# A joined change: 256-key neighbourhood units, transposed router logits, one second matrix loaded ahead of its ring

## Chip, core and metric

The program runs on one core of a Trainium2 chip, in one launch. The metric is the device time of that launch in microseconds. TensorE is called PE, VectorE DVE, ScalarE ACT, GpSimd POOL and SyncE SP. Everything is 32-bit float. The core has 16 DMA engines, which all queues share.

## What is computed

A first block on 512 tokens of width 1024 (normed attention of two kinds, an output projection, a mixture of 32 experts, a side path), and then two more layers with a context of 256 tokens, which the change doesn't touch. What matters here, cut from the reference:

```python
ob = neighbourhood_attention(...)   # 16 heads of 32; 8 rows of 64 columns; a query sees all 8 rows,
    kb = np.minimum(cs[:, 0], GRID_W - K_COLS)      # K_COLS = 32 columns per block of 16 query columns
    key_cols = kb[:, None] + np.arange(K_COLS)[None, :]
    col_valid = ((key_cols[:, None, :] >= cs[:, :, None]) & (key_cols[:, None, :] < cs[:, :, None] + WIN_C))
    sc = einsum(qb, kg) * scale + bias;  pr = softmax(sc);  o = einsum(pr, vg)
h = h + concatenate([oa, ob]) @ w_out
g_prob = softmax(xf @ w_rg);  g_gate, g_idx = top_k(g_prob, 1)      # 4 groups
e_logits = (xf @ w_re)[group g_idx];  e_w, e_i = top_k(softmax(e_logits), 2)   # 8 experts in each
hdn = silu(xb @ w1[e]) * (xb @ w3[e]);  y = hdn @ w2[e]             # 1024 x 512, 1024 x 512, 512 x 1024
h = h + rms_norm(p @ w_ple, g_ple) * sigmoid(rms_norm(h, g_plg) @ w_plg)
```

## The kernel before

The tokens are ordered so that one tile of 128 tokens is a block of 16 grid columns by 8 rows; there are XT = 4 tiles. The first layer (`first_layer`, tensors named `mix_...`) runs in stages, and each engine has its instructions written out by hand in one list, with semaphores between the lists.

**Attention.** The class `Attention` writes one attention for all engines. A unit is one tile of queries of one group of heads. PE's list for iteration n (`tensor`): scores of unit n+LEAD, where a group begins soon its turned q and k (L338), transposes of unit n's weights (L377, in pieces of four tiles), a turned output of the first attention (`extra`, L403), turned inverses of a group that has closed (L411), values of unit n-1 (L391; L394 in the first attention). DVE (`vector`) takes each head's maximum with the bias added (L504), copies every piece but the first (L208) and finishes a group. ACT (`scalar`) copies the first piece (L208), then makes the exponentials of unit n+LEAD, one per head (L587), then empties an extra (L454). Three PSUM banks go round for all that is turned. `diff` is the first attention (16 units of 512 keys, LEAD 2, two score maps), `near` the neighbourhood attention: four groups of four heads, 16 units, LEAD 1. Its units of tiles 0 and 3 see two tiles of keys (256), those of tiles 1 and 2 three tiles (384). The bias blocks, which also mask the columns outside the window, are built by POOL from the padded table (`shifted`), written to `bias_blocks` in HBM by ACT's queue, and read by SP's queue into EM, two groups' worth of room, 8 transfers a group (L897, `table_in`).

**Behind it.** PE projects with w_out (L1031), turns h (L1041), multiplies by the router's matrix (`route`, L1047: the turned h of a tile is stationary, w_router's 36 columns move), and does pieces of the side product p @ w_ple (`beside`, L1085, eight of two products each) between the ranking (L1092, L1094) and the two slot lists (L1103). DVE scales the logits (L1591) and chooses groups and experts (L1616 to L1631). POOL gathers expert rows (L1901) and scatters results (L1908).

**Experts.** 31 experts run in a fixed loop, the last and any overflow in a dynamic one (one trip here). PE's list for expert e: first product w1 (L1138), hidden of e-1 turned (L1143), product w3 (L1138), rows of e+1 turned (L1131), second product of e-1 with w2 (L1150). Each matrix has 2 MB. SP loads them in the order of use into six places, `use_of(which, e) % PLACES`; a load waits until the matrix six uses back has been read. The sixth place is the tensor `sixth` and part of `consts`, in three transfers (L920 to L922); others take one (L924). From expert 7 on pieces of the context layer run along, for which ACT's queue loads 12 x 0.5 MB. What the change touches of the memory: `base` (EM, and the context's rows in the same range), `work` (q, k, weights, later the router's h), `sixth`, and the place of the side norm (`own`, `side_gain`).

Below, w1(e), w3(e), w2(e) are an expert's matrices.

## Time and profile before

| | us |
|---|---|
| median of three runs | 1813.12 (1813.02 to 1815.79) |
| the profiled execution | 1818.79 |
| its span | 1817.0 |
| input projection, to 205.6 | 205.6 |
| first attention | 48.7 |
| neighbourhood attention, 254.3 to 320.5 | 66.2 |
| output projection | 55.5 |
| router and slot lists | 35.4 |
| experts, 411.4 to 920.1 | 508.7 |
| the two later layers | 896.9 |
| PE busy over the span | 1752.2 (96%) |

In the page, the span is cut into 40 slices of 45.4 us: transfers move 393 to 419 GB/s in the eleven slices from 409 to 908 us and at most 286 elsewhere. PE busy is modelled from pipelined matmuls, so 96% doesn't say that it can't go faster; what it waits for is read in its waits and in the timeline. The clock column (PEclk) is the share of 2.4 GHz that was granted; 0.50 means 1.2 GHz.

### The profile page before, as it was taken

The page shows a single profiled execution, that of the slowest core. Times are in us where ns is not written, and L with a number is a line of the kernel's source. Part 1 is how long each engine was busy: PE and PEld are TensorE (multiplying, and loading weights), DVE is VectorE, ACT ScalarE, POOL GpSimd, SP SyncE. Part 2 cuts the span into 40 slices and gives each one's busy share as a digit, 9 for nine tenths or more (in the row PEclk, how much of TensorE's full clock was granted, in tenths as well). Part 3 has the DMA queues.
Part 4 walks back from the last instruction along what each step waited for, and adds up shares of the span by engine and source line. Part 5 has one row for each costly group of instructions (what it writes and reads, how often), then busy time and mean ns, then how long its engine had stood idle before and what let it go on. Part 6 is the DMA issues. An engine that isn't in the chain of part 4 may idle for free. (4 is left out here: it accounts for less than half of the span.)

```text
span 1817.0 us, 24698 instructions
## 1 busy us (share of the span) xinstructions
PE 1752.2 (96%) x9850; PEld 971.7 (53%) x9850; DVE 748.2 (41%) x1591; ACT 555.0 (31%) x1121; POOL 153.8 (8%) x194
## 2 busy tenths in 40 slices
PE   8999988999999899999989999999999999999998
PEld 3443455465544444555474444577745644566663
DVE  2344477132511221333223315477624337566642
ACT  2111477123101111333223212355412233444420
POOL 0310000001111010111100014000000001100000
PEclk9999999989999999999999999999999999999999
DMA  8664688439999999999971222000110012100001
GB/s 282 229 223 185 94 163 117 165 124 393 417 416 416 415 416 417 418 417 419 409 286 47 93 93 93 1 2 1 36 73 35 24 41 74 43 1 2 2 24 47
DMA packets 94594, 324.86 MB, mean 179 GB/s; under 512 B 12792, under 2 KB 31224, under 8 KB 69392
## 3 DMA queue, kind: packets, MB, share of 16 engines
q1 hardware_dynamic: 80624, 302.55, 45.7%
q10 hardware_dynamic: 8656, 12.32, 2.0%
q0 software_dynamic: 5200, 8.41, 1.3%
q8 instruction: 79, 1.29, 0.3%
q14 instruction: 35, 0.29, 0.1%
HBM read 317.58 MB, written 14.30 MB: 183 GB/s over the span
## 5 line engine op out<-in xcount | busy, mean ns | idle before, releaser
L2228 PE MATMUL tail_ps<-arena 128*128 128x512 f32 x488 | 213.3, 592 | 0.0
L1138 PE MATMUL mix_ps<-arena 128*64 128x256 f32 x1568 | 181.8, 385 | 8.3 <-DMA arena<-in_w 5.8
L1014 PE MATMUL mix_ps<-arena,side 128*128 128x512 f32 x384 | 171.1, 603 | 1.2 <-DMA arena<-in_w_in 0.6
L500 DVE TENSOR_SCALAR_CACHE_REDUCE arena<-tail_ps 128x768 f32<-128x768 f32 x128 | 117.5, 955 | 114.2 <-PE tail_ps L358 69.8
L2228 PEld LDWEIGHTS tail_ps<-arena 128*128 128x128 f32 x488 | 91.8, 190 | 110.3 <-issue 109.9
L1138 PEld LDWEIGHTS mix_ps<-arena 128*64 128x64 f32 x1568 | 110.3, 138 | 70.3 <-issue 11.8
L1150 PE MATMUL mix_ps<-arena 128*64 128x512 f32 x512 | 116.9, 598 | 18.9 <-DMA arena<-in_w 18.3
L1014 PEld LDWEIGHTS mix_ps<-arena,side 128*128 128x128 f32 x384 | 72.7, 192 | 97.4 <-issue 94.9
L2228 PE MATMUL tail_ps<-arena,side 128*128 128x512 f32 (+2 forms) x328 | 123.6, 535 | 0.0
L587 ACT ACTIVATE arena<-arena,tail_small 128x768 f32<-128x768 f32 x128 | 118.0, 926 | 6.4 <-DVE arena L500 6.4
L377 PE MATMUL tail_ps<-first,arena 128*128 128x128 f32 x768 | 97.9, 277 | 0.5 <-ACT arena L587 0.5
L377 PEld LDWEIGHTS tail_ps<-first,arena 128*128 128x128 f32 x768 | 82.7, 140 | 28.1 <-issue 26.8
L2228 PEld LDWEIGHTS tail_ps<-arena,side 128*128 128x128 f32 x328 | 61.9, 190 | 58.1 <-issue 47.4
L1400 ACT ACTIVATE arena<-mix_ps,mix_small 128x512 f32<-128x512 f32 x31 | 21.3, 687 | 226.2 <-PE mix_ps L1150 226.2
L1684 DVE COPY arena<-mix_ps 128x256 f32<-128x256 f32 x31 | 13.1, 424 | 180.3 <-PE mix_ps L1143 180.2
L2228 PE MATMUL tail_ps<-side,arena 128*128 128x512 f32 x184 | 80.4, 592 | 0.0
L1150 PEld LDWEIGHTS mix_ps<-arena 128*64 128x64 f32 x512 | 34.1, 136 | 78.8 <-issue 55.5
L1908 POOL DMA_INDIRECT expert_out<-arena,mix_indices x31 | 31.5, 1016 | 413.7 <-ACT arena L1400 407.3
L1336 ACT ACTIVATE arena<-mix_ps,mix_small 128x512 f32<-128x512 f32 x24 | 16.2, 687 | 149.9 <-PE mix_ps L1014 128.5
L2228 PEld LDWEIGHTS tail_ps<-side,arena 128*128 128x128 f32 x184 | 34.9, 190 | 43.5 <-issue 43.5
L1138 PE MATMUL mix_ps<-sixth,arena 128*64 128x256 f32 x450 | 54.8, 382 | 0.6 <-issue 0.6
L1031 PE MATMUL mix_ps<-arena,side 128*128 128x512 f32 x128 | 55.3, 592 | 0.0
(411 smaller groups left out, 2458.5 us busy)
## 6 DMA issues: line engine op xcount, KB each, us to landing
arena<-in_w SPq DMA_DIRECT2D x81, 2048.0 KB, 18.3
arena<-in_l_w_mod SPq DMA_DIRECT2D x16, 1024.0 KB, 6.5
arena<-in_l_w_in SPq DMA_DIRECT2D x16, 1024.0 KB, 7.2
sixth<-in_w SPq DMA_DIRECT2D x15, 1024.0 KB
sixth<-in_w SPq DMA_DIRECT2D x15, 896.0 KB
arena<-in_w_in SPq DMA_DIRECT2D x12, 1024.0 KB, 9.2
arena<-in_l_w_mod SPq DMA_DIRECT2D x16, 512.0 KB, 6.1
residual<-bias_blocks SPq DMA_DIRECT2D x32, 224.0 KB, 12.2
```

The source lines that it names most:

```text
L377: ins = pe.transpose(Tp[:, bank, z * P:(z + 1) * P], pr[:, n % self.PRB, x, kt * P:(kt + 1) * P], m["ident"])
L500: dve.tensor_scalar(self.rows_of(n, x), self.scores_of(n, x), -1.0, None, ALU.mult, ALU.min, accum_out=nm[:, b, x:x + 1]).then_inc(s["maxe ...
L587: act.activation(pr[:, b, x, 0:k], in_, ACT.Exp, bias=nm[:, b, x:x + 1], scale=scale, accum_out=sm[:, og_b, z, x:x + 1]).then_inc(s["exped ...
L1014: last = pe.matmul(ps[:, u % 4], oT[:, k, t * P:(t + 1) * P], weights.slot(W_IN[n, k // 4], 4, 512)[:, k % 4], start=(k == 0), stop=(k == ...
L1031: last = pe.matmul(ps[:, u % 4], oT[:, k, t * P:(t + 1) * P], weights.slot(W_OUT[cc, k // 4], 4, 512)[:, k % 4], start=(k == 0), stop=(k = ...
L1138: last = pe.matmul(out[h * CAP:(h + 1) * CAP, 0:H2], x, block_of(k, h), start=(k == 0), stop=(k == DK - 1))
L1150: last = pe.matmul(py[h * CAP:(h + 1) * CAP, :], x, wb[:, f, h * 512:(h + 1) * 512], start=(f == 0), stop=(f == FK - 1))
L1336: act.activation(proj[:, t, cc * 512:(cc + 1) * 512], ps[:, (XT * n + t) % 4], ACT.Copy, scale=rs_x[:, t:t + 1]).then_inc(s["in_ev"], 1)
L1400: act.activation(yb[:, e % 2], py, ACT.Copy, scale=gate_w[:, e:e + 1]).then_inc(s["y_out"], 1)
L1684: dve.tensor_copy(hT.rearrange("p j q -> p (j q)"), ph[:, 0:2 * P]).then_inc(s["h_taken"], 1)
L1908: pool.indirect_dma_start(out=y_rows, out_offset=bass.IndirectOffsetOnAxis(ap=index[:, 1, e:e + 1], axis=0), in_=yb[:, e % 2], in_offset=N ...
L2228: last = pe.matmul(out, lhs(k), rhs(k), start=(k == 0), stop=(k == K - 1))
```

## The change

- **Units of 256 keys.** The units of tiles 1 and 2 take the half tile on either side and their own tile, 256 keys instead of 384. The keys are read in place by a strided pattern (`near_keys`); their scores are made in two products of 128 keys for each head (`cut`). The outer halves of the values are put together beforehand by 32 transfers of 8 partitions x 512 on SP's queue (`mixed`), for which the second unit's values wait. A bias table has 24 blocks instead of 28.
- **Order inside the attention.** ACT makes the exponentials of n+1 ahead of the copy of n's weights (`ahead`). The first group's q and k are turned inside the first attention, at its unit 14 (`turns_after`). The turned outputs come at units 7, 8, 11, 12 instead of 5, 7, 9, 11.
- **Tables.** The third group's table goes into the sixth place and no longer waits for the first group; the fourth waits for the first group's maxima. w1(2), which goes into the sixth place too, is loaded behind the third group's maxima.
- **Router.** w_router is stationary and h moves: one product chain for tiles 0 and 1, one for each of tiles 2 and 3; DVE copies the logits (36 partitions), PE turns them, DVE scales them in one instruction.
- **Side product.** Piece 5 stands behind the second slot list; pieces 6 and 7 stand in expert 0 behind its third step.
- **Ring.** w2(1) is loaded once into `once`, outside the ring, right behind the router's norms; the context's rows follow. The order of use is a list (`asked`), so the odd place is now filled by w3 of even experts. The side norm (own squares, gain) runs one expert later, its row `g_ple` is loaded at expert 4.

The diff, cut to its core:

```diff
@@ Attention
-            cuts = [(a, min(hi - lo, a + 4)) for a in range(0, hi - lo, 4)]
+            cuts = [(a, min(hi - lo, a + self.cut(t))) for a in range(0, hi - lo, self.cut(t))]
...
+        if turns_after is not None:
+            self.turn_step[turns_after[0]] = (self.groups, range(len(turns_after[1])))
...
+            if self.ahead and n + LEAD < self.N:
+                exponential(n + LEAD)
             if n < self.N:
                 self.empty_weights(act, 1, n)
-            if n + LEAD < self.N:
+            if not self.ahead and n + LEAD < self.N:
                 exponential(n + LEAD)
...
@@ first_layer
+    bias_at = [EM[:, 0], EM[:, 1], view(sixth, 0, 24, P), EM[:, 0]]
+    TABLE_IN = ((0, 2), (0, 2), (1, 1), (0, 3))
...
+    def near_keys(g, x, t, lo, hi):
+
+        rows_of_head = slice(32 * x, 32 * x + 32)
+        if not middle(t):
+            first = 0 if t == 0 else (XT - 2) * P
+            return kT[rows_of_head, g % 2, first + (lo - 2 * t) * P:first + (hi - 2 * t) * P]
+        if lo == 2 * t + 1:
+            return kT[rows_of_head, g % 2, t * P:(t + 1) * P]
+        both = view(work, 1024 + g % 2 * SEQ + (t - 1) * P + CB // 2, 2, 2 * P - CB // 2)[rows_of_head, :, 0:P]
+        return both.rearrange("p h (r c) -> p h r c", c=CB)[:, :, :, 0:CB // 2].rearrange("p h r c -> p r h c")
...
             for g in range(2):
                 table_in(g)
+            sp.wait_ge(s["in_ev"], 24)
+            for t in range(1, XT - 1):
+                for half in range(2):
+                    for r in range(ROWS):
+                        to, of = r * CB + half * (CB // 2), r * CB + (1 - half) * (CB // 2)
+                        sp.dma_start(mixed[to:to + CB // 2, t - 1], proj[of:of + CB // 2, t - 1 + 2 * half, 2560:3072]).then_inc(s["mixed_in"], 16)
             for i in range(W_OUT[0, 0], W_PLE + 1):
                 weights.load(sp, i)
-            for g in range(2, 4):
-                sp.wait_ge(s["near_maxed"], near.first_of[g - 1] * 4)
-                table_in(g)
+            table_in(2)
+            sp.wait_ge(s["near_maxed"], near.first_of[1] * 4)
+            table_in(3)
...
-            sp.wait_ge(s["shifted"], 1)
+            sp.wait_ge(s["near_maxed"], near.first_of[3] * 4)
             expert(2, "w1")
...
             expert(1, "w3")
+            sp.wait_ge(s["h_squared"], 2 * XT)
+            expert(1, "w2")
+            for b in range(2):
+                sp.wait_ge(s["spilled"][b], 32)
+            sp.dma_start(hx[:, XT:AT], A["ctx"].rearrange("(t p) d -> p t d", p=P)).then_inc(s["ctx_in"], 16)
             sp.wait_ge(s["listed"], 2)
             expert(0, "w2")
...
+            def route(i):
+                lo, hi = route_parts[i]
+                pe.wait_ge(s["h_gained"], hi)
                 for k in range(DK):
-                    last = pe.matmul(ps[:, t, 0:N_GROUPS + N_EXPERTS], h_in[:, k, t * P:(t + 1) * P], wr[:, k], start=(k == 0), stop=(k == DK - 1))
+                    last = pe.matmul(ps[0:WIDTH, i, 0:(hi - lo) * P], wr[:, k], h_in[:, k, lo * P:hi * P], start=(k == 0), stop=(k == DK - 1))
+                last.then_inc(s["logits"], 1)
...
                 if e:
                     second(e - 1)
+                else:
+                    beside(6)
+                    beside(7)
```

In the order of instructions, three places. ACT's list inside the neighbourhood attention, one group from its turned keys to its first output. L587 and L595 are exponentials, L208 copies what PE turned, L454 and L461 empty a turned output of the first attention. Before:

```order
L208 ACTIVATE arena<-mix_ps 128x512 x2
L587 ACTIVATE arena,mix_small<-arena,mix_small 128x256 x4
L208 ACTIVATE arena<-mix_ps 128x512
L587 ACTIVATE arena,mix_small<-arena,mix_small 128x256 x4
L454 ACTIVATE side<-mix_ps,mix_small 128x512
L208 ACTIVATE arena<-mix_ps 128x512
L587 ACTIVATE arena,mix_small<-arena,mix_small 128x384 x4
```

After:

```order
L208 ACTIVATE arena<-mix_ps 128x512 x2
L595 ACTIVATE arena,mix_small<-arena,mix_small 128x256 x4
L208 ACTIVATE arena<-mix_ps 128x512
L595 ACTIVATE arena,mix_small<-arena,mix_small 128x256 x4
L208 ACTIVATE arena<-mix_ps 128x512
L461 ACTIVATE side<-mix_ps,mix_small 128x512
L595 ACTIVATE arena,mix_small<-arena,mix_small 128x256 x4
```

The alternation reads the same, but a copy is now that of the unit before the exponentials above it, not of the one whose exponentials follow; and no row has 384 keys.

PE's list from the last turning of h to the first expert. L1047 and L1105 are the router's products, L1111 the turned logits, L1085 and L1149 the side product, L1103 and L1167 the slot lists, L1131 and L1193 an expert's rows, L1138 and L1200 its first products. Before, first the router and then, further down, the lists:

```order
L1041 MATMUL mix_ps<-first,residual 128x128 x16
L1047 MATMUL mix_ps<-arena 128x36 x16
L1041 MATMUL mix_ps<-first,residual 128x128 x8
L1047 MATMUL mix_ps<-arena 128x36 x16
L1085 MATMUL mix_ps<-arena,extra 128x512 x6
...
L1103 MATMUL mix_ps<-arena 128x32 x8
L1085 MATMUL mix_ps<-arena,extra 128x512 x4
L1103 MATMUL mix_ps<-arena 128x64 x8
L1085 MATMUL mix_ps<-arena,extra 128x512 x4
L1131 MATMUL mix_ps<-first,arena 128x128 x4
```

After:

```order
L1098 MATMUL mix_ps<-first,residual 128x128 x16
L1105 MATMUL mix_ps<-arena 36x256 x8
L1098 MATMUL mix_ps<-first,residual 128x128 x8
L1105 MATMUL mix_ps<-arena 36x128 x16
L1111 MATMUL mix_ps<-first,arena 128x36 x4
...
L1149 MATMUL mix_ps<-arena,extra 128x512 x2
L1167 MATMUL mix_ps<-arena 128x64 x8
L1149 MATMUL mix_ps<-arena,extra 128x512 x2
L1193 MATMUL mix_ps<-first,arena 128x128 x4
L1200 MATMUL mix_ps<-arena 64x256 x32
L1193 MATMUL mix_ps<-first,arena 128x128 x4
L1149 MATMUL mix_ps<-arena,extra 128x512 x4
```

Two side products left the space between the lists, two that before the first rows, and four products (pieces 6 and 7) stand behind the second expert's turned rows.

SP's queue from the first tables on. Before:

```order
L897 DMA residual<-bias_blocks 16x28x128 x16
L650 DMA arena<-in_w_out 128x4x512 x4
L650 DMA arena<-in_w_ple 128x2x1024
L897 DMA residual<-bias_blocks 16x28x128 x16
L920 DMA sixth<-in_w 128x2048
...
L936 DMA residual<-in_l_b_gate 128x1024 x3
L924 DMA arena<-in_w 128x2x2048 x3
L947 DMA arena<-in_g_ple 128x1024
L924 DMA arena<-in_w 128x2x2048 x2
L953 DMA residual<-in_ctx 128x2x1024
```

After:

```order
L942 DMA residual<-bias_blocks 16x24x128 x16
L955 DMA residual<-arena 8x512 x32
L661 DMA arena<-in_w_out 128x4x512 x4
L661 DMA arena<-in_w_ple 128x2x1024
L942 DMA sixth<-bias_blocks 16x24x128 x8
L942 DMA residual<-bias_blocks 16x24x128 x8
...
L990 DMA residual<-in_l_b_gate 128x1024 x3
L978 DMA arena<-in_w 128x2x2048 x2
L967 DMA arena<-in_w 128x2x2048
L998 DMA residual<-in_ctx 128x2x1024
L978 DMA arena<-in_w 128x2x2048 x6
```

The 32 rows of `mixed` stand ahead of w_out, the tables' third group has another target, w2(1) (L967) and the context's rows stand ahead of w2(0), and `g_ple` has moved out of sight.

## Rows read from the trace of the kernel before

**Rows 1.** By stretch: us, busy PE PEld DVE ACT POOL, clock, DMA share, GB/s.

```profile
254.30:320.50 66.20, 53.14 (x664) 36.85 (x665) 50.40 (x171) 52.14 (x162) 6.48 (x8) 0.97 0.71 101
320.50:376.00 55.50, 55.50 (x138) 25.08 (x137) 9.13 (x25) 9.06 (x13) 0.00 (x0) 1.00 0.38 145
376.00:411.40 35.40, 35.40 (x165) 25.50 (x164) 15.92 (x56) 8.36 (x14) 2.22 (x2) 0.81 0.45 163
411.40:497.70 86.30, 84.14 (x607) 46.68 (x606) 36.81 (x107) 22.57 (x34) 12.79 (x12) 1.00 1.01 410
497.70:703.30 205.60, 186.69 (x1146) 95.27 (x1146) 38.47 (x98) 22.84 (x38) 25.12 (x24) 1.00 1.02 415
703.30:892.40 189.10, 185.96 (x1276) 103.80 (x1276) 60.44 (x117) 63.97 (x126) 23.52 (x23) 1.00 1.01 416
```

**Rows 2.** PE's waits on transfers, whole span: us in total, times, longest.

```profile
PE mix_ps L1150 <- DMA arena<-in_w: 18.3, 15, 1.8
```

**Rows 3.** Timeline, neighbourhood stage: start, us, engine, line, operands, count, [idle <-releaser].

```profile
286.29 0.71 PE L365 MATMUL mix_ps<-arena 32*128 32x256 f32 x8
...
302.22 0.71 PE L365 MATMUL mix_ps<-arena 32*128 32x256 f32 x8
...
303.84 0.42 DVE L504 CUSTOM_DVE_ANT_0 arena<-mix_ps,residual 128x256 f32<-128x256 f32 x1
...
305.09 0.49 ACT L587 ACTIVATE arena<-arena,mix_small 128x256 f32<-128x256 f32 x1
...
306.23 1.09 PE L377 MATMUL mix_ps<-first,arena 128*128 128x128 f32 x8 [0.18 <-ACT arena L587]
...
306.98 0.60 ACT L208 ACTIVATE arena<-mix_ps 128x512 f32<-128x512 f32 x1 [0.23 <-PE mix_ps L377]
...
307.25 0.65 PE L391 MATMUL mix_ps<-arena 128*32 128x128 f32 x16
...
308.07 0.60 ACT L587 ACTIVATE arena<-arena,mix_small 128x384 f32<-128x384 f32 x1
```

**Rows 4.** Timeline of PE between the two attentions.

```profile
252.43 1.04 PE L338 MATMUL mix_ps<-first,arena 128*128 128x128 f32 x8
254.32 0.71 PE L365 MATMUL mix_ps<-arena 32*128 32x256 f32 x8 [0.86 <-ACT arena L208]
```

**Rows 5.** Timeline of the router's products and the choice of experts.

```profile
378.06 3.69 PE L1047 MATMUL mix_ps<-arena 128*128 128x36 f32 x32
...
383.30 6.88 PE L1047 MATMUL mix_ps<-arena 128*128 128x36 f32 x32
...
390.51 0.17 DVE L1616 TENSOR_REDUCE arena<-arena 128x4 f32<-128x16 f32 x1
...
395.54 0.29 DVE L1631 TENSOR_TENSOR arena<-mix_small 128x128 f32<-128x128 f32 x1
...
397.81 0.43 PE L1092 MATMUL mix_ps<-arena,consts 128*128 128x160 f32 x2
```

**Rows 6.** By stretch, the router's place (columns as in the first group).

```profile
381.00:395.00 14.00, 14.00 (x53) 11.15 (x53) 5.90 (x26) 2.10 (x3) 0.00 (x0) 0.52 0.63 258
```

**Rows 7.** Timeline of the slot lists, the first gather and the first expert.

```profile
404.30 1.22 POOL L1901 DMA_INDIRECT arena<-expert_in,mix_indices  x1 [84.40 <-DVE mix_indices L1654]
...
406.14 1.89 PE L1103 MATMUL mix_ps<-arena 128*128 128x64 f32 x16
...
411.37 0.63 PE L1131 MATMUL mix_ps<-first,arena 128*128 128x128 f32 x4
```

**Rows 8.** Timeline of SP's queue: start, us until the last is issued, transfers.

```profile
206.66 24.81 SPq L897 DMA_DIRECT2D residual<-bias_blocks  x16
...
408.07 0.37 SPq L924 DMA_DIRECT2D arena<-in_w  x1
...
416.49 3.82 SPq L924 DMA_DIRECT2D arena<-in_w  x2
```

**Rows 9.** By stretch, the first two tables' transfers (columns as in the first group).

```profile
210.00:220.00 10.00, 8.39 (x54) 5.38 (x53) 9.22 (x21) 7.72 (x20) 0.00 (x0) 1.00 1.28 106
```

More of the change, by code:

```diff
@@ L342, in scores @@
             g, t, lo, hi, _, _ = units[n]
[L343 removed]
+            if n == self.first_of[g] and not (g == 0 and self.turned_before):
                 dve_n, act_n = self.emptied_by([("turn", g, j) for j in range(len(turns[g]))])
@@ L540, in divide @@
             dve.tensor_tensor(o, o, Tp[:, r % 3, lo:hi], ALU.mult).then_inc(s["emptied_dve"], 1)
-        self.empty_turn(dve, 0, 0, range(between[0]) if between else None)
+        if not self.turned_before:
+            self.empty_turn(dve, 0, 0, range(between[0]) if between else None)
         if between:
@@ L588, in exponential @@
                                accum_out=sm[:, og_b, z, x:x + 1]).then_inc(s["exped"], 1)
-        self.empty_turn(act, 1, 0, range(between[0]) if between else None)
+        if not self.turned_before:
+            self.empty_turn(act, 1, 0, range(between[0]) if between else None)
         if between:
@@ L672, in first_layer @@
     oT = view(side, 0, DK, SEQ)
-    EM = view(base, late, 2, 28, P)
+    EM, mixed = view(base, late, 2, 24, P), view(base, late + 2 * 24 * P, 2, 512)
     sq, tw = view(base, late, 2, 512), view(base, late + 1024, 2, 8, 64)
@@ L782, in first_layer @@
     split = lambda which, e: use_of(which, e) % PLACES == PLACES - 1
-    assert all(which == "w1" for which in ("w1", "w3", "w2") for e in range(STATIC) if split(which, e))
+    assert all(which != "w2" for q, (which, _) in enumerate(asked) if q % PLACES == PLACES - 1)
     H2, last_half = D_EXPERT // 2, m["masks"][:, 0:D_EXPERT // 2]
@@ L837, in first_layer @@
     banks = dict(S=ps[:, 0:4].rearrange("p b n -> p (b n)"), T=ps[:, 4:7], O=ps[:, 7])
+    near_turns = [[(tiles_of(1536 + g * P), P, [qT[:, g % 2]]), (tiles_of(2048 + g * P), P, [kT[:, g % 2]])] for g in range(4)]
     def diff_first(what):
@@ L853, in first_layer @@
                      lambda h, x, kt: proj[:, kt, 1024 + h * P:1024 + (h + 1) * P], P, combine=neg_lam, rows_to=on,
-                     ready={k: diff_first(k) for k in ("ring", "scores", "output")})
+                     ready={k: diff_first(k) for k in ("ring", "scores", "output")}, turns_after=(len(units) - 2, near_turns[0]))
     def near_first(what):
@@ new lines, in near_values @@
+    def near_values(g, x, chunk):
+        t = chunk // 2
+        at = slice(g * P + x * NA_D, g * P + (x + 1) * NA_D)
+        if middle(t) and chunk % 2 == 0:
+            return mixed[:, t - 1, at]
+        tile = t if middle(t) else chunk % 2 + (0 if t == 0 else XT - 2)
+        return proj[:, tile, 2560:3072][:, at]
+    near = Attention(nc, m, sem_of("near_"), dict(banks, pr=view(work, pr_at, 2, 4, 2 * P), pT=view(work, pT_at, 2, 8, P), nm=nm_n, sm=sm_n, rc=rc_n, ratio=None,
+                                                  wide=wide),
+                     [(g, t, 2 * t, 2 * t + 2, g, t) for g in range(4) for t in range(XT)], 4, 1,
+                     near_turns,
+                     4, lambda g, x, t, lo, hi: (qT[32 * x:32 * x + 32, g % 2, t * P:(t + 1) * P], near_keys(g, x, t, lo, hi)),
+                     near_values, NA_D, lambda g: oT[:, 4 + g], cut=lambda t: 1 if middle(t) else 2, ahead=True,
+                     bias=dict(loaded=lambda g: (s["table_in"][TABLE_IN[g][0]], 16 * ROWS * TABLE_IN[g][1]), of=near_table),
+                     turned_before=True,
+                     extra={(7, 8, 11, 12)[h]: ([proj[:, t, h * P:(h + 1) * P] for t in range(XT)], oT[:, h], sub_gain, (s["o_scaled"], h + 1)) for h in range(4)},
@@ L1388, in _, with take_side @@
             act.wait_ge(s["out_mm"], 2 * XT)
-            for u in range(2 * XT):
+            def take_side(u):
+                act.wait_ge(s["side_mm"], u + 1)
+                act.activation(side[:, u * 512:(u + 1) * 512], ps[:, 5 + u % 3], ACT.Copy).then_inc(s["side_ev"], 1)
+            for u in range(2 * XT - 2):
                 if u == 2:
```

150 lines of the change are left out of this document (82 added, 68 removed).

## Prediction

> **What bounds the kernel now.** I read the busy times by stretch first [rows 1]. Four stretches matter. From 254.3 to 320.5 us (neighbourhood attention) no engine is full: PE 53, DVE 50 and ACT 52 of 66 us, so a chain of short steps through all three sets the pace. From 320.5 to 376.0 (output projection) PE is busy 55.5 of 55.5 us. From 376.0 to 411.4 (router, slot lists) PE reads as busy too, but at a mean clock of 0.81. From 411.4 to 892.4 (experts) the transfers run at 410 to 416 GB/s without a break, while PE has room: it waits for the second matrix 15 times, 18.3 us in total [rows 2]. So the experts are bound by bytes; a microsecond won ahead of them moves them all, and a byte taken out of them is worth its time at 416 GB/s. After them nothing differs in the change, and I carry the shift through to the end.
>
> **Neighbourhood units, 384 keys to 256.** Eight of 16 units lose a third of their keys. Per unit that is ACT 4 x (0.60 - 0.49) us of exponentials (a 256-key one starts every 0.49 us, a 384-key one every 0.60) and 4 of 12 transposes [rows 3]. That alone, as a floor for the gain, is 8 x 0.44 = 3.5 us. The larger part is the order on ACT. Before, ACT copies the turned weights of unit n ahead of unit n+1's exponentials, so it stands still from its last exponential to PE's first four transposes: 306.23 to 306.98 in the row, about 0.8 us a unit. A group of four units takes 302.22 - 286.29 = 15.9 us [rows 3], and ACT's own list gives nearly that: 2 x (2.4 + 0.8 + 0.6) + 2 x (2.0 + 0.8 + 0.6) + one turned key copy 0.55 + one normed output 0.67 = 15.6. After, the exponentials of n+1 fill that gap. What is late next is PE's own order: scores of n+1, transposes of n, values of n-1. Two units close one round: first score to maximum 0.7, maximum to exponential 0.45, four exponentials 2.05, a copy between 0.6, eight transposes 1.0, values 0.57 [rows 3], and 0.3 of hand-overs that I estimate from the idle figures in those rows: 5.65 us, or 2.8 a unit. The turned q and k (1.0), the turned output and the inverses (about 0.5 each) lie on PE besides: 4 x 2.8 + 2.1 = 13.3 us a group, against 15.9. Four groups are 10.4; the drain at the end is not shortened, so I take 10.0. If ACT alone were the bound (4 x (1.96 + 0.6) + 1.2 = 11.5), it would be 17.7. The eight score products of 128 keys that replace four of 384 in a middle unit have no row; the columns fall by a third, the instructions double. I take 0.7 to 0.9 us against 0.93, and it changes the group by under 0.3.
>
> **First turning ahead.** The eight transposes at 252.43 stand between the last values of the first attention and the first scores at 254.32 [rows 4]. After, they run two units earlier, where PE waits for DVE; their two copies delay that unit's tail by 0.3 us or so. Gain 1.9 - 0.3 - 0.3 = 1.3 us. Near stage together: **-11.3**, between -4.8 and -19.
>
> **Tables and mixed values on SP's queue.** SP gets 32 small transfers that build the middle units' values, ahead of w_out. Sixteen table transfers take SP 24.81 us, 1.55 each [rows 8], and their 512-byte pieces move at 106 GB/s [rows 9]; they become six sevenths as large, so two tables are issued by 228 and a table of 1.57 MB takes 14.8 us. Most of the 1.55 is the queue pushing back on 3.7 MB, and the small ones hold 0.5 MB together, so I take 0.4 us each (a whole matrix was issued in 0.37 at 408.07 [rows 8]). They end near 228 + 13 = 241, and are asked for by the second unit's values, near 257. w_out and w_ple (5.2 MB, 13 us) follow, then the third table without a wait, there by 270; needed at 253 + 26.6 = 280. The fourth waits for the first group's maxima near 267 and is there by 285; needed at 293. I cost this at nothing; without that cover every late microsecond counts in full. The Trainium skill, DMA: Bandwidth & Descriptors, section on the anatomy of one DMA, gives about 2.0 us of fixed cost to a transfer; one after the other that would be 64 us for the 32 and would speak against this change, but it puts most of it down to the completion's way back, which transfers issued in a row share. No row here shows transfers between two places of the same memory.
>
> **Router with transposed logits.** Before, 64 instructions of 36 columns take 3.69 and then 6.88 us, the second half at a clock of 0.52 on average, 1.2 GHz instead of 2.4 [rows 5, 6]; the side products behind them are slow as well and hold the ranking product back to 397.81, though DVE has its last input at 395.83 [rows 5]. After, h moves and w_r stays: 8 products of 256 columns and 16 of 128. The projection's 64 products of 512 columns take 55.5 us less one turning, 0.85 each [rows 1], so these cost 3.4, 1.7 and 1.7. Starting at 378.7 with one turning (1.0) between, they end near 386.5; copies, four small turnings and one scaling add 1.0. DVE's choice starts at 387.5 instead of 390.51, lasts 5.3, and the ranking follows at once at 393.1 instead of 397.8: **-4.7**. This needs the clock to stay up. It fell near 381, behind transposes and 36-column products; products with seven and three and a half times the columns now take their place. If it falls all the same, the products end near 391.6, the ranking comes at 399, and the term is +1.
>
> **Slot lists and the side products.** One side product (1.8 us) less stands ahead of the second list, so w2(0) is issued 1.6 us earlier than 408.07, relative to the ranking; two more leave the path to the first turning at 411.37, which comes 3.0 earlier. The gather issued at 404.30 has 4.0 us until then, with no other transfer under way; no row shows when it was in, only that it was by 411.37 [rows 7], so at worst the 3.0 is lost. The two side products now stand in expert 0 after its third step: 3.7 us of PE. PE has 18.3 us to spare later, so this costs only if it lets the transfers run dry.
>
> **Bytes out of the stream.** w2(1) (2.10 MB) and ctx (1.05 MB) now load while PE works at the router, when the transfers are busy only 0.45 of the time [rows 1]. 3.15 MB at 417 GB/s is 7.5 us. Against it: the 0.52 MB of the side gain lay in an idle gap before w3(2) at 416.49 [rows 8] and now costs 1.25; and I find two new gaps, before w3(3) (its place is freed 2.8 us later, by the side products) and before w1(5), 1.7 us together. For it: w2(0) 1.6 and w3(2) another 1.3 earlier. Sum **-7.5**, between -5 and -9. By the Trainium skill, DMA: Bandwidth & Descriptors, section Specifications, HBM gives a core about 358 GB/s, and the 3.15 MB would be worth 8.8 us, a sum 1.3 us larger; the rows show 410 to 416 over 480 us, so here the measured rate decides.
>
> The rest (the third group's blocks in the sixth place, w1(2) later, the side norm one expert later, late_at's new places) has its time: w1(2) still lands before the projection ends, the side norm has no reader for hundreds of microseconds. Costed at nothing.
>
> **Sum.** -11.3 - 4.7 - 7.5 = -23.5. The profiled execution took 1818.8 us (span 1817.0), the median of three is 1813.1; the former is 0.3% slow throughout, so I subtract from the median: 1813.1 - 23.5 = **1789.6 us**; a profiled span would read 1793.5.
>
> **Rivals.** (a) The clock falls in the router all the same: +1 instead of -4.7, 1795.3. For: the turnings ahead are the same. Against: the columns. (b) ACT's order gives nothing, because the exponentials now wait for maxima that DVE makes no sooner: -4.8 instead of -11.3, 1796.1. Against: DVE's four maxima need 1.4 us of a unit's 2.8. (c) The transfers run dry: after the earlier start, places are freed by PE, not waited for by it, and the 7.5 is lost, 1797.1. For: from 703.3 to 892.4 PE is busy 186 of 189 us [rows 1], so there both bounds lie together. Against: DMA share is 1.01 there as well. (d) Slower: each of the 32 small transfers takes 1.55 us like the tables' [rows 8]. Then the mixed values come at 228 + 50 = 278 instead of 257, w_out and w_ple (13) and the table itself (15) bring the third table at 306 and the fourth at 321, and the last group ends 17 us behind it, at 338, 17.5 later than now: +17.5 - 4.7 - 7.5 = +5.3, 1818.4. It begins to cost above 0.9 us each. (e) ACT is the only bound: -17.7 - 1.3 for the near stage, 1781.9.
>
> **How the numbers follow.** Forecast 0.58, (a) 0.12, (b) 0.11, (c) 0.09, (d) 0.04, (e) 0.03, and 0.03 for small losses that meet. The range reaches to (b) and (c) together with 3 us of spread and on the other side half way to (e): 1783 to 1801. About 0.2% (3.6 us) is what a measurement here can tell from no change. Faster is all but (d) and the last: 0.93; same 0.03; slower 0.04.
>
> **What would show it.** Right: a group of near units in 13 to 13.6 us; the first scores right behind the first attention's last values; clock 1.00 through the router; ranking 4 to 5 us earlier after the last projection; DMA share 1.0 from the first w3(2) to the end of the experts and that stretch 7 us shorter from the lists on. Wrong: PE waiting for the bias table or for mixed values between 255 and 300; idle transfers between 415 and 460; a half clock between 376 and 395; or a gain ahead of 411 that is gone at 892.

## The result and the profile after

| | median us | lowest to highest | runs | against before (95% interval) |
|---|---|---|---|---|
| before, first group of runs | 1813.5 | 1813.0 to 1815.8 | 4 | |
| changed kernel, first group | 1793.7 | 1791.7 to 1796.3 | 4 | 0.9889 (0.9870 to 0.9908) |
| changed kernel, second group (after_again) | 1792.9 | 1791.0 to 1796.0 | 4 | 0.9890 (0.9875 to 0.9905) |
| changed kernel, third group (after_third) | 1793.4 | 1790.8 to 1797.4 | 4 | 0.9891 (0.9862 to 0.9921) |

The change makes the kernel 19.8 us faster, 1.1%; 23.5 us were forecast. The profiled execution of the changed kernel took 1796.3 us with a span of 1794.5; a span of 1793.5 was forecast from before's 1817.0. So the spans differ by 22.5 us and the medians by 19.8, and that difference turns out to be the most instructive part of the case.

The span can be cut at four events of PE's timeline: the first scores of the neighbourhood attention, the first product of the output projection, the ranking product of the router and the first context output product (the first after the experts). In us; before_again is a second trace of the kernel before, from the experiments below:

| trace | to first scores | neighbourhood attention | projection and router | lists and experts | rest | span |
|---|---|---|---|---|---|---|
| before | 254.3 | 66.2 | 77.3 | 522.2 | 897.0 | 1817.0 |
| before_again | 254.0 | 67.9 | 71.4 | 522.3 | 896.8 | 1812.3 |
| after | 251.7 | 60.5 | 72.9 | 512.7 | 896.8 | 1794.5 |
| after_again | 251.5 | 58.3 | 72.9 | 512.2 | 896.9 | 1791.8 |
| after_third | 251.1 | 59.8 | 72.9 | 512.8 | 896.7 | 1793.3 |

The stretches of the changed kernel that answer to [rows 1], by window: us, busy PE PEld DVE ACT POOL, clock, DMA share, GB/s. They are the neighbourhood attention, projection, router and lists, and three stretches of experts.

```profile
251.70:312.20 60.50, 47.44 (x634) 35.01 (x634) 42.10 (x164) 48.25 (x162) 6.49 (x8) 0.94 0.89 163
312.20:368.00 55.80, 55.80 (x139) 25.09 (x138) 9.14 (x24) 9.06 (x13) 0.00 (x0) 1.00 0.38 144
368.00:395.30 27.30, 26.26 (x143) 17.17 (x142) 16.31 (x56) 7.28 (x12) 2.23 (x2) 1.00 0.78 301
395.30:480.00 84.70, 83.92 (x585) 45.83 (x586) 30.70 (x85) 22.62 (x35) 12.79 (x12) 1.00 1.00 403
480.00:682.90 202.90, 191.48 (x1178) 97.57 (x1174) 44.72 (x120) 23.98 (x39) 25.13 (x24) 0.99 1.02 415
682.90:872.00 189.10, 186.15 (x1276) 104.16 (x1276) 60.89 (x118) 63.96 (x126) 23.52 (x23) 1.00 1.01 416
```

Against [rows 1]: the neighbourhood attention is 6 us shorter though its clock is lower (0.94, it was 0.97); router and lists take 27.3 us at full clock instead of 35.1 (from 376.3) at 0.81; they move 301 GB/s instead of 163, the bytes taken out of the experts. The experts still run at 415 GB/s. PE's waits on the second matrix [rows 2] fell from 18.3 to 10.4 us (waits of the changed kernel, from the lists to the end of the experts):

```profile
PE mix_ps L1212 <- DMA arena<-in_w: 10.4, 10, 1.7
```

**In the neighbourhood attention** something new stands. SP's queue (timeline: start, us until the last is issued, transfers), DVE's timeline and PE's and ACT's right behind it:

```profile
205.80 18.71 SPq L942 DMA_DIRECT2D residual<-bias_blocks  x16
224.56 23.39 SPq L955 DMA_DIRECT2D residual<-arena  x32
247.99 2.80 SPq L661 DMA_DIRECT2D arena<-in_w_out  x4
...
252.82 17.33 SPq L942 DMA_DIRECT2D sixth<-bias_blocks  x8
...
282.69 0.42 DVE L511 CUSTOM_DVE_ANT_0 arena<-mix_ps,sixth 128x256 f32<-128x256 f32 x1 [3.98 <-DMA sixth<-bias_blocks]
...
285.85 1.89 PE L384 MATMUL mix_ps<-first,arena 128*128 128x128 f32 x8 [0.92 <-ACT arena L208]
```

The 32 mixed transfers took SP 0.73 us each, not the 0.4 of the forecast; w_out is issued at 248.0 instead of 241, the third table is in at 282.7 instead of 270, and DVE waits 4.0 us for it. Behind the wait the clock is down: eight transposes take 1.89 us, 1.09 at full clock [rows 3].

**In the router** PE's timeline reads:

```profile
367.98 1.91 PE L1098 MATMUL mix_ps<-first,residual 128*128 128x128 f32 x16
370.43 3.62 PE L1105 MATMUL mix_ps<-arena 128*36 128x256 f32 x16 [0.53 <-DVE arena L1656]
373.97 1.09 PE L1098 MATMUL mix_ps<-first,residual 128*128 128x128 f32 x8
375.00 3.68 PE L1105 MATMUL mix_ps<-arena 128*36 128x128 f32 x32
378.61 0.69 PE L1111 MATMUL mix_ps<-first,arena 36*128 36x36 f32 x4
379.24 5.42 PE L1149 MATMUL mix_ps<-arena,extra 128*128 128x512 f32 x12
385.08 0.54 PE L1156 MATMUL mix_ps<-arena,consts 128*128 128x160 f32 x2 [0.43 <-DVE arena L1704]
```

The ranking stands 17.1 us behind the first turning of h (L1098), 21.5 before (376.3, where that turning starts, to 397.8 in [rows 5]); the clock stays up, as forecast.

### The profile page after: what moved, and what is told of

The parts are those of the page before. It is cut to its first block and busy times, and to the rows that moved or that the text cites. A ratio compares the mean times of both kernels' runs of the same rounds, so it can differ in the third digit from the quotient of the medians.

```text
span 1794.5 us, 24625 instructions
## 1 busy us (share of the span) xinstructions
PE 1740.3 (97%) x9806; PEld 962.4 (54%) x9806; DVE 739.8 (41%) x1583; ACT 551.0 (31%) x1121; POOL 152.5 (8%) x192
## 3 DMA queue, kind: packets, MB, share of 16 engines
q8 instruction: 78, 1.28, 0.3%
## 5 line engine op out<-in xcount | busy, mean ns | idle before, releaser
L1200 PE MATMUL mix_ps<-arena 128*64 128x256 f32 x1568 | 180.1, 382 | 3.3 <-DVE arena L1750 1.7
L1200 PEld LDWEIGHTS mix_ps<-arena 128*64 128x64 f32 x1568 | 110.2, 137 | 70.7 <-issue 18.8
L1212 PE MATMUL mix_ps<-arena 128*64 128x512 f32 x512 | 118.6, 606 | 13.6 <-DMA arena<-in_w 10.4
L595 ACT ACTIVATE arena<-arena,tail_small 128x768 f32<-128x768 f32 x128 | 118.0, 926 | 6.4 <-DVE arena L507 6.4
L1200 PE MATMUL mix_ps<-sixth,arena 128*64 128x256 f32 x450 | 55.0, 382 | 0.3 <-DMA consts<-in_w 0.3
## 6 DMA issues: line engine op xcount, KB each, us to landing
arena<-in_l_w_mod SPq DMA_DIRECT2D x16, 512.0 KB, 6.4
arena<-in_l_w_in ACTq DMA_DIRECT2D x12, 512.0 KB, 10.6
```

The source lines that it names most:

```text
L595: act.activation(pr[:, b, x, 0:k], in_, ACT.Exp, bias=nm[:, b, x:x + 1], scale=scale, accum_out=sm[:, og_b, z, x:x + 1]).then_inc(s["exped ...
L1200: last = pe.matmul(out[h * CAP:(h + 1) * CAP, 0:H2], x, block_of(k, h), start=(k == 0), stop=(k == DK - 1))
L1212: last = pe.matmul(py[h * CAP:(h + 1) * CAP, :], x, wb[:, f, h * 512:(h + 1) * 512], start=(f == 0), stop=(f == FK - 1))
```

## The experiments

### Is the third table's wait what the attention lost?

**after_again** and **after_third** are the changed kernel once more.

> The changed kernel as it is, beside the runs of this call. Span 1790 to 1795, neighbourhood stage (first scores to first output product) 60.5 us with a wait of 4.0 us for the third table near 282.7. If that wait belongs to one execution only, it is absent here and the stage is 55.5 to 57.

> The changed kernel as it is, once more, beside the next one. Span 1790 to 1795, a wait of 0.9 to 4.0 us for the third table.

Measured: spans 1791.8 and 1793.3, attention 58.3 and 59.8 us; the wait was 2.1 us in after_again. In after_third DVE stands still for 1.9 us at the same place; the trace puts that down to PE, whose scores had been done for 1.5 us. Three traces further down have the changed kernel's attention too: beside_back, both_stream and route_36 waited 2.6, 1.0 and 0.9 us for this table, and their attention took 57.6, 55.9 and 57.1 us. So the third table is late each time, but by 0.9 to 4.0 us.

**third_first**: the third table ahead of w_out.

```
+table_in(2)
 for i in range(W_OUT[0, 0], W_PLE + 1):
     weights.load(sp, i)
-table_in(2)
 sp.wait_ge(s["near_maxed"], near.first_of[1] * 4)
```

> The changed kernel with the third table issued ahead of w_out and w_ple instead of behind them. If the 4.0 us wait for the third table, and the half clock behind it, are what the stage lost against the forecast: the table is there by 265, the wait is gone, the stage lasts 55 to 56.5 us instead of 60.5 and the kernel is 4 to 5 us faster than the changed one. The fourth table is then issued behind w_out's transfers; it comes between 283 and 291 and is needed near 291, so up to 2 us of wait can come back there. If the wait only hides another chain (ACT's exponentials), the stage stays above 59 and the time is that of the changed kernel within 1 us.

Measured: 1791.6 us, ratio 0.9882 (0.9866 to 0.9897), 1.3 less than after_again beside it (0.9890, 0.9875 to 0.9905). The wait is gone, as expected, but the attention took 57.4 us, more than the 55 to 56.5, and the gain is a third of what was expected; the intervals overlap, so the times alone don't show it. **mixed_pool** (run again as **mixed_pool_again**) goes one step further: POOL issues the mixed transfers.

```
 # SP
-sp.wait_ge(s["in_ev"], 24)
-... 32 x sp.dma_start(mixed...)
+table_in(2)
 for i in range(W_OUT[0, 0], W_PLE + 1):
 ...
 # POOL, ahead of its wait for inv_o
+pool.wait_ge(s["in_ev"], 24)
+... 32 x pool.dma_start(mixed...)
```

> The 32 mixed transfers are issued by POOL instead of SP, and the third table ahead of w_out. If the 32 transfers' 23 us on SP (0.73 each against the 0.4 forecast) are what made everything behind them late: SP issues the third table at 224.5, no wait for any table, stage 55 to 56.5 us, 4 to 5 us faster than the changed kernel, and 0 to 2 us faster than with the third table ahead alone. If POOL takes over 1.5 us for each of them, they end after 254, and the first values near 259 wait for them: the stage is longer by what they are late.

> The 32 mixed transfers on POOL and the third table ahead of w_out, once more: no wait over 0.5 us for a table, neighbourhood stage 55 to 57.5 us by how often the clock falls in it, 1.5 to 3 us faster than the changed kernel.

Measured: 1791.0 and 1792.0 us, 1.9 and 1.5 less than the changed kernel in the same groups; the attention took 55.4 us in both traces, inside the expected range. The lowest times of this study, but by 0.1% only and with overlapping intervals (0.9883 against 0.9890, 0.9884 against 0.9891), less than can be told apart in one group; that both groups point the same way is all there is for it. POOL's timeline shows 31 of the 32 at 0.52 us each (the last one was issued 14.7 us behind them, at 232.4), and SP's the third table right behind the first two:

```profile
201.68 16.02 POOL L1967 DMA_DIRECT2D residual<-arena  x31 [80.71 <-ACT arena L1395]
...
232.66 14.97 SPq L942 DMA_DIRECT2D sixth<-bias_blocks  x8
```

What separates the attention of third_first from that of mixed_pool, 2.0 us with no wait of more than 0.3 us for a table in either, goes with the clock: third_first has two stretches of half clock, mixed_pool one. (By its first scores third_first is 1.3 us ahead, by the first output product 0.7 behind.) The windows of third_first (first two rows) and of mixed_pool (last two), columns as above:

```profile
252.00:258.00 6.00, 4.63 (x47) 3.95 (x48) 4.11 (x20) 5.00 (x20) 0.00 (x0) 0.72 1.27 113
264.00:270.00 6.00, 3.37 (x36) 2.46 (x36) 2.65 (x12) 5.66 (x19) 4.03 (x4) 0.76 1.03 344
```

```profile
258.00:264.00 6.00, 5.54 (x64) 4.07 (x56) 4.48 (x19) 5.97 (x21) 0.00 (x0) 0.87 1.05 358
264.00:270.00 6.00, 3.76 (x66) 2.44 (x64) 3.70 (x16) 5.97 (x20) 3.87 (x4) 1.00 1.05 393
```

In third_first the clock falls again at 267. Just before, ACT loads its function table for the square root and then the one for the exponentials, 1.28 us each, and PE waits 2.6 us for it. That wait alone doesn't explain the fall: in mixed_pool PE waits 2.2 us at the same place and in after 2.3, and there the clock stayed up; it had fallen a little later the first time. One stretch of half clock in this stage goes with about 2 us by this one pair, and every trace of the study has one to four of them. That the issue of the mixed transfers had anything to do with it is not shown.

### The order on ACT and the keys

**ahead_off** undoes the order alone, **before_ahead** does the order alone.

```
-... cut=lambda t: 1 if middle(t) else 2, ahead=True,
+... cut=lambda t: 1 if middle(t) else 2, ahead=False,
```

> The changed kernel with ACT's old order: the copy of a unit's turned weights ahead of the next unit's exponentials. If the order was the larger part of the stage's gain: ACT's list sets the pitch again, 2.0 + 0.8 + 0.6 = 3.4 us a unit instead of 3.0, a group 14.8 instead of 13.3; the wait for the third table takes up part of it (the table lands at 282.7 all the same), so the stage is 2 to 6 us longer than 60.5 and the kernel 2 to 6 us slower than the changed one. If the order gives nothing (rival b): the stage stays at 60.5 within 1 us.

Measured: 1797.3 us, ratio 0.9915 (0.9901 to 0.9928), 4.4 more than after_again; attention 61.5 us with no wait for a table. Against third_first, which has none either and as many stretches of half clock (two), the order is worth 61.5 - 57.4 = 4.1 us. PE's and ACT's timeline of ahead_off, one unit:

```profile
301.11 0.50 ACT L595 ACTIVATE arena<-arena,mix_small 128x256 f32<-128x256 f32 x1
...
303.08 0.67 ACT L461 ACTIVATE side<-mix_ps,mix_small 128x512 f32<-128x512 f32 x1
303.23 1.09 PE L384 MATMUL mix_ps<-first,arena 128*128 128x128 f32 x8 [0.60 <-ACT arena L595]
303.98 0.60 ACT L208 ACTIVATE arena<-mix_ps 128x512 f32<-128x512 f32 x1 [0.23 <-PE mix_ps L384]
304.47 0.50 ACT L595 ACTIVATE arena<-arena,mix_small 128x256 f32<-128x256 f32 x1
```

Here ACT's exponentials are 3.36 us apart (301.11, 304.47); in third_first, same place, 3.0. Over the whole stage the difference is smaller: from the first scores to the last it is 53.5 us in ahead_off and 50.7 in third_first, 0.2 us a unit, and from the last scores to the first output product 8.0 and 6.7. So the old order costs 0.2 us a unit and 1.3 more at the drain, not 0.8 a unit. The gap that the forecast counted is partly filled by another copy (L461). That was so before the change as well; ACT's row in the very gap of [rows 3]:

```profile
306.07 0.67 ACT L454 ACTIVATE side<-mix_ps,mix_small 128x512 f32<-128x512 f32 x1
```

From 306.23 to 306.98 ACT was busy with this for 0.5 us; it waited 0.23, as its next row in [rows 3] says. In other units of before the same wait is 0.8 to 1.2 us.

```
 for n in range(self.N + 1):
+    if self.bias is not None and n + LEAD < self.N:
+        exponential(n + LEAD)
     if n < self.N:
         self.empty_weights(act, 1, n)
-    if n + LEAD < self.N:
+    if self.bias is None and n + LEAD < self.N:
         exponential(n + LEAD)
```

> The kernel before with one edit: in the neighbourhood attention ACT takes the exponentials of the next unit ahead of the copy of this unit's turned weights (the first attention as it was); keys stay 256 and 384. If the order alone is worth what it was worth in the changed kernel without a table's wait (61.5 - 57.4 = 4.1 us): the stage is 62 instead of 66.2 us and the kernel 3.5 to 5 us faster than before. If PE's twelve transposes and 24 value products of a 384-key unit take ACT's place as the bound, it is 0.5 to 2.5 us. If the order is worth more with long exponentials, 6 to 7 us.

Measured: 1820.2 us, ratio 1.0036 (1.0020 to 1.0053): slower, against all three expectations; the attention takes 73.4 us instead of 66.2, with half clock in four places. ACT's and PE's timeline of before_ahead, one unit of 384 keys:

```profile
276.82 0.61 ACT L587 ACTIVATE arena<-arena,mix_small 128x384 f32<-128x384 f32 x1 [0.61 <-DVE mix_small L504]
...
278.63 0.60 ACT L587 ACTIVATE arena<-arena,mix_small 128x384 f32<-128x384 f32 x1
279.23 0.57 ACT L208 ACTIVATE arena<-mix_ps 128x512 f32<-128x512 f32 x1
279.86 0.66 PE L403 MATMUL mix_ps<-first,arena 128*128 128x128 f32 x4 [2.49 <-ACT arena L208]
...
281.89 1.24 PE L365 MATMUL mix_ps<-arena 32*128 32x256 f32 x8
```

A unit of 384 keys turns into three pieces of PSUM, and there are three banks for turned things. ACT now copies its piece out only behind the next unit's four exponentials; PE needs that bank for the turned output (L403) and waits 2.5 us for it, and behind L403 stand the values and the next scores. A unit of 256 keys has two pieces and leaves a bank. So the order needs the keys' cut: by trace, keys and order as before 66.2, order alone 73.4, new units alone 61.5, both 57.4 us (55.4 in mixed_pool). These four hold one, four, two and two stretches of half clock. The wait of 2.5 us comes three times in before_ahead (it ends at 279.9, 298.4 and 317.0), and each time the clock is down right behind it or at its end; so part of the 7.2 us is clock, and how much each has was not run apart.

### The router: the operands' order or the clock

**route_36** is the changed kernel with the old products.

```
 def route(t):
-    last = pe.matmul(ps[0:WIDTH, i, 0:(hi - lo) * P], wr[:, k], h_in[:, k, lo * P:hi * P], ...)
+    last = pe.matmul(ps[:, t, 0:WIDTH], h_in[:, k, t * P:(t + 1) * P], wr[:, k], ...)
-for i in range(3):
-    turn_logits(i)
```

> The changed kernel with the router's products of before: h stands, w_r moves, 36 columns each. If the order of the operands is what kept TensorE's clock up and took 4.4 us out (first output product to ranking 72.9 us in the changed kernel, 77.3 before): that stretch is 77 us again, the granted clock from 372 to 386 is near 0.5, and the kernel is 4 to 4.5 us slower than the changed one. If the clock stayed up for another reason (what PE did before the stage, the transfers), the clock is 1.0 and the stretch is 73.5 to 74.5 us.

Measured: in the trace just what the first theory says, 77.3 us from the first output product to the ranking, with half clock from 368.9 on. But the median is 1796.3 us with a ratio of 0.9890 (0.9861 to 0.9919), the changed kernel's own, though 4 us more would still lie within the interval, and its four runs are 1789.4, 1795.8, 1796.7 and 1797.5: one lies 6 us below the rest. PE's timeline of route_36 (three rows) and of before_again, the same instructions:

```profile
365.35 3.66 PE L1104 MATMUL mix_ps<-arena 128*128 128x36 f32 x32
368.85 1.75 PE L1098 MATMUL mix_ps<-first,residual 128*128 128x128 f32 x8
370.39 6.88 PE L1104 MATMUL mix_ps<-arena 128*128 128x36 f32 x32
```

```profile
379.48 3.66 PE L1047 MATMUL mix_ps<-arena 128*128 128x36 f32 x32
382.97 1.07 PE L1041 MATMUL mix_ps<-first,residual 128*128 128x128 f32 x8
383.88 3.66 PE L1047 MATMUL mix_ps<-arena 128*128 128x36 f32 x32
387.37 5.40 PE L1085 MATMUL mix_ps<-arena,extra 128*128 128x512 f32 x12
393.27 0.54 PE L1092 MATMUL mix_ps<-arena,consts 128*128 128x160 f32 x2 [0.50 <-DVE arena L1631]
```

**before_again** is the kernel before, for a second trace.

> The kernel before as it is, for a second trace. Its first trace had a span of 1817.0 us where its other runs lie near 1813.5. If that execution was 0.3% slow throughout, this one has every stage 0.3% shorter: neighbourhood stage 66.0 instead of 66.2, first output product to ranking 77.1 instead of 77.3, ranking to the first context output product 520.7 instead of 522.2, the rest 894.5 instead of 897.0, span near 1811.5 to 1813. If single places differ from execution to execution (stretches of half clock), most stages are equal within 0.1 us and one or two are 2 to 4 us apart.

Measured: 1812.5 us (ten runs), span 1812.3. The attention is 1.8 us longer, with a wait of 1.9 us for a bias table; the other stretches are equal within 0.3 us, but for the router, which is 6.0 us shorter: here the clock never fell, on the same list of instructions. The second theory holds. The old products have two router times, 71.4 us in this trace and 77.3 in the other three (before, before_ahead, route_36); the new ones had 72.9 in all ten traces that have them. So the new router gains 4.4 us where the clock would have fallen, and loses 1.6 where it would not, by the one trace in which it did not: its products end 0.9 us later after the first output product (66.5 against 65.6), and the ranking, with the turned logits in between, comes 6.4 instead of 5.7 us behind them. The second product is half as long at full clock in before_again as in [rows 5], 3.66 against 6.88 us. The Trainium skill, TensorE: Matmul & The Clock Gate, says in Part 1 (What's actually happening) that the chip's look at PE's activity runs free of the kernel, so that the same instructions meet it at another point each time; these two traces agree. Why the clock held for the 256- and 128-column products in ten traces of ten, no run shows.

### The experts: bytes or PE

**both_stream** issues w2(1) and ctx in the stream; **beside_back** puts two side products ahead of the first expert.

```
-expert(1, "w2")                         # ahead of the slot lists
-... ctx
 for e in range(2, STATIC):
     ...
     if e == 2:
+        expert(1, "w2")
+        ... ctx
         continue
```

> The changed kernel with w2(1) and ctx issued behind w3(2), in the stream of the experts, instead of ahead of the lists; their places and readers are the same. If the experts are bound by bytes: ranking to the first context output product takes 512.4 + 3.15 MB / 417 GB/s = 512.4 + 7.5 = 520 us, and the kernel is 7 to 8 us slower than the changed one. If the transfers had room (the gain of 9.8 us there came from the side products' order and the gaps), it is 0 to 3 us slower.

Measured: ranking to the first context output product 518.7 us, 5.9 to 6.5 more than the changed kernel's 512.2 to 512.8; 1800.3 us, ratio 0.9926 against 0.9890, which is 6.5 us. The bytes are worth about 6.3 of their 7.5.

```
 list_slots(..., s["hot"], s["listed"])
 beside(5)
+beside(6)
+beside(7)
 ...
-else:                                   # expert 0
-    beside(6)
-    beside(7)
 ...                                     # ACT's two copies of them move too
```

> The changed kernel with the last two side products ahead of the first expert again, instead of inside it. If bytes bound the experts and PE has room: the first turning comes 3.5 us later after the ranking (13.8 instead of 10.2 us), the second product of expert 0 at the same time as now within 0.3 us, and the first context output product 512.4 us after the ranking within 0.5: no change. If PE's start is what moved the experts, the kernel is 2 to 3.5 us slower.

Measured: the first turning comes 3.4 us later after the ranking (13.7 instead of 10.2), but the second product of expert 0 only 0.8 (32.0 us, 31.2 in after; 0.3 was expected), and the first context output product 514.0 us behind the ranking, 1.2 to 1.8 more. The time is 1793.6 us, ratio 0.9884 (0.9864 to 0.9904), no difference that the times show. The trace has a longer stretch of half clock near 483 us than after's, but mixed_pool, third_first and turn_late have the same one there and took 512.0 to 512.5 us. So the clock at that place doesn't account for the 1.2 to 1.8 us, and some of them may be the side products'; all of the 3.5 it is not.

### The first turning

**turn_late** drops one argument each of the two attentions (turns_after, turned_before).

```
- ... turns_after=(len(units) - 2, near_turns[0]))
+ ... )
-                     turned_before=True,
```

> The changed kernel with the first q and k of the neighbourhood attention turned between the two attentions again. By the forecast's term: the first scores come 1.9 - 0.3 - 0.3 = 1.3 us later, at 252.8 to 253.5 instead of 250.9 to 252.2, and the kernel is 1.3 us slower; the table's wait takes up to 1.3 of that back, so 0 to 1.5. If the turning was hidden before as well, no change.

Measured: the first scores come at 253.8, 1.6 to 3.1 later than in the ten traces with the turning ahead (250.7 to 252.2), the wait for the table is gone, as expected, and the time is 1794.0 us, ratio 0.9893 (0.9871 to 0.9915): the same as the changed kernel's. In the changed kernel the earlier start runs into the late table: the first scores of route_36 come 1.2 us ahead of those of both_stream, and both take up the third table at 279.9. What the earlier start is worth without that wait was not run.

## Why the prediction was right, and where it was not

**Neighbourhood attention, forecast -11.3.** To the first output product, the two traces of before have 320.5 and 321.9, the three of the changed kernel 312.2, 309.8 and 310.9: -10.2 on the means. With beside_back, both_stream and route_36, whose attention is the same, the six average 309.6: -11.6. The size is right, the parts are not. The pitch was right, by PE's timeline of after, the scores of the twelfth unit and of the sixteenth:

```profile
292.16 0.71 PE L372 MATMUL mix_ps<-arena 32*128 32x256 f32 x8
...
305.46 0.71 PE L372 MATMUL mix_ps<-arena 32*128 32x256 f32 x8
```

That is 13.3 us for four units, as forecast; from the ninth unit to the thirteenth it is 13.0 in third_first and in mixed_pool. The split was wrong: the forecast gave the keys a floor of 3.5 us and called the order the larger part, with 0.8 us a unit. By ahead_off and third_first the keys and the rest of the new units brought 4.7 and the order 4.1, where 3.5 and 6.5 were forecast; from the ninth unit's scores to the thirteenth's it is 15.9 us before, 13.6 in ahead_off, 13.0 in third_first. And the first scores came 2.7 us earlier on the means, not 1.3. That these parts, less the table's wait, add up to the forecast's size is luck. The misreading is in the 0.8 us: it was taken from a gap in which ACT waited 0.23. And the order is no part of its own; without the keys' cut the stage took 7.2 us more. The prediction didn't see this, since its argument looked at ACT's list alone and not at the bank that ACT's copy frees. "The drain at the end is not shortened" failed too, in the kernel's favour: from the last scores to the first output product it is 6.7 us, 7.9 before.

**"I cost this at nothing"** (tables and mixed values) failed. The term was 0.4 us for each of 32 transfers; 0.73 was measured, and with 13 us of w_out in front the third table came at 282.7 in after instead of 270, 0.9 to 4.0 us late over six traces. The forecast said that it begins to cost above 0.9 us each. That is the limit for the mixed values (asked for near 257); for the third table its own terms, 228 + 32 x + 13 + 15 = 280, give 0.75, and 0.73 is at that limit. What made the table late even so is that its bytes, and not only its issue, stand behind those of w_out and w_ple, which fill the transfers from 252 to 264; the table's follow at about 100 GB/s until past 280 (windows of after):

```profile
252.00:258.00 6.00, 3.82 (x44) 2.89 (x44) 4.10 (x18) 4.67 (x18) 0.00 (x0) 0.77 1.05 392
258.00:264.00 6.00, 5.54 (x76) 3.87 (x68) 4.47 (x20) 5.95 (x21) 0.00 (x0) 0.95 1.06 370
264.00:270.00 6.00, 3.62 (x60) 2.48 (x52) 3.88 (x18) 5.99 (x20) 4.03 (x4) 1.00 1.27 98
...
276.00:282.00 6.00, 5.19 (x67) 3.69 (x65) 1.89 (x6) 3.04 (x10) 0.00 (x0) 1.00 1.27 112
```

It is the mechanism of rival (d), with a wait of 0.9 to 4.0 us where (d) had 17.5, and third_first and mixed_pool take the wait away.

**Router, forecast -4.7.** Right for the trace it was read from (-4.4 by route_36 and by the first pair of traces), and, as far as the runs tell, wrong as a term of the median. The failed step is the sentence "the former is 0.3% slow throughout, so I subtract from the median". The profiled execution was slow in one place, in the router, by 6.0 us. The medians seem to be those of executions without this loss: before's five groups have 1812.1 to 1815.4, and only 7 of their 49 runs lie above 1816, while the profiled execution took 1818.8. Which of the timed runs lost time in the router is not recorded, so this is inferred. Against executions without the loss the new router is 1.6 us slower, +1.6 in place of -4.7. Rival (a) had nearly the size of the other case (+1) with the wrong mechanism: it is not the changed kernel whose clock falls, it is before's that sometimes doesn't. This is where the 3.7 us between 23.5 and 19.8 went, and the lists' larger gain, below, gave some back; that the total still fell close to the forecast is in part luck. The first pair of traces differs by 22.5 us, before_again and after_again, both with full clock in the router, by 20.5.

**Lists and stream, forecast -7.5, measured -9.4 to -10.1.** Just past the bound of -9. The 3.15 MB were put at 7.5 less 2.95 for the side gain and new gaps plus 2.9 for earlier issues; both_stream shows about 6.3 for the bytes. What the forecast had not at all is the end: from the last regular second product to the first context output product before takes 27.6 and 27.3 us, the changed kernel 25.7. The product with w3 in the dynamic loop's trip waits less there, and the clock holds. Before and after:

```profile
909.29 5.36 PE L1138 MATMUL mix_ps<-arena 128*64 128x256 f32 x32 [2.91 <-DMA arena<-in_w]
```

```profile
887.33 3.67 PE L1200 MATMUL mix_ps<-arena 128*64 128x256 f32 x32 [1.37 <-DMA arena<-in_w]
```

The shorter wait is 1.5 us of it and the clock 1.4 to 1.7 (5.06 us for these products in before_again), and 1.3 us go back on a new wait ahead of the context's first product: 1.6 to 1.9 us in all. The places of late_at were "costed at nothing"; whether they or the order of the last transfers shortened the wait, and whether the clock would have held without it, was not run apart. Rival (c), that the gain is lost between 703 and 892, is out: the shift is 20.4 us at 703 and 20.4 at 892. Rival (b) is out by ahead_off, (e) by the pitch.

## What to carry to other kernels

A saving read at a place of half clock is no term of a median until a second execution shows the same clock there; two traces of the unchanged kernel would have shown that it moves. An order of instructions on one engine is worth what the buffers that it holds let through: count the banks before and after, not only the engine's idle time. Small transfers queued ahead of large ones cost their issue time to everything behind them, so put them where nothing waits behind them. Bytes taken out of a stretch that is bound by transfers came back for the most part (6.3 of 7.5 us), while 3.4 us of PE's work moved out of the way of that stretch showed as at most 1.8 us in the trace and not in the times.

## What the runs showed of the hardware

The granted clock is not a property of the list of instructions. The router of before ran at 1.2 GHz in one execution and at 2.4 in the next, 6.0 us apart, and the neighbourhood attention met one to four stretches of half clock at changing places in all fourteen traces, about 2 us each by the one pair that could be compared. Nineteen runs of the kernel before spread over 8.6 us (1808.7 to 1817.2) in one group; the four of mixed_pool spread over 2.7.

The time in which SP issues a set of transfers says little of the set: the same eight transfers of the third table took 17.3 us behind w_out (after), 4.9 behind the small ones (third_first) and 15.0 behind the first two tables (mixed_pool). The 32 transfers of 16 KB within the same memory took 0.73 us each to issue on SP; on POOL, 31 of them took 0.52 each and the last came 14.7 us later. The Trainium skill, DMA: Bandwidth & Descriptors, says in its Rules for kernel authors that spreading transfers over issuing engines saves only issue time; here that was all that was wanted. Together with the third table's earlier place it went with 1.5 and 1.9 us in the medians, which the intervals do not set apart from nothing.
